# Last layer norm of a MoE transformer block: gain and bias moved from GpSimd to VectorE, row statistics from VectorE to ScalarE

## What is computed

```python
x1 = layer_norm(DEEPNORM_ALPHA * x + merged @ w_out[i], ln1_g[i], ln1_b[i])
y = hier_moe(x1, ...)     # y[token] = w0 * expert0(x1[token]) + w1 * expert1(x1[token])
ple = (p[i] @ w_ple[i]) * jax.nn.sigmoid(x1 @ w_ple_gate[i] + ple_gate_b[i])
x = layer_norm(DEEPNORM_ALPHA * x1 + y + ple, ln2_g[i], ln2_b[i])
# layer_norm: (x - mean) * rsqrt(mean((x - mean)^2) + 1e-5) * g + b, over the 1024 columns of a row
```

## Time and profile before

| what | value |
|---|---|
| median of 3 runs | 2067.24 us (2064.98 to 2072.45) |
| span of the profiled execution | 2062.2 us, first to last instruction |
| median of the runs less that span | 5.0 us |
| TensorE busy | 1806.4 us (88%) |
| VectorE busy | 1059.5 us (51%) |
| ScalarE busy | 826.6 us (40%) |
| GpSimd busy | 304.1 us (15%) |

### The profile page before, as it was taken

How to read it: one execution, slowest core, us unless ns; L and a number is a source line. 1 busy time by engine, 2 the same in 40 slices (tenths; PEclk the granted TensorE clock), 3 DMA queues, 4 the chain that set the end, 5 groups by cost and what they waited for, 6 DMA issues and landing times.

```text
span 2062.2 us, 27399 instructions
## 1 busy us (share of the span) xinstructions
PE 1806.4 (88%) x8478; PEld 1452.6 (70%) x8478; DVE 1059.5 (51%) x1307; ACT 826.6 (40%) x1077; POOL 304.1 (15%) x335
## 2 busy tenths in 40 slices
PE   7999999999988898989897898789888899899830
PEld 6888888888865586868676676677677677677720
DVE  2015655500125544243446634776776776777737
ACT  3132233211234313131213213666766766767621
POOL 0112212110100010000000120012221222111217
PEclk9999999999977898999999999899999999999965
DMA  6242333222423234242224266678878878888663
GB/s 233 87 118 106 121 115 114 98 78 92 150 98 116 94 114 142 92 158 92 87 104 136 81 209 250 269 314 342 358 305 349 348 309 362 329 333 360 263 239 128
DMA packets 100534, 396.62 MB, mean 192 GB/s; under 512 B 17921, under 2 KB 25345, under 8 KB 88194
## 3 DMA queue, kind: packets, MB, share of 16 engines
q1 hardware_dynamic: 77778, 319.45, 41.0%
q0 software_dynamic: 22704, 76.49, 9.8%
HBM read 331.01 MB, written 64.94 MB: 192 GB/s over the span
## 4 chain that ended last, share of the span: by engine, by line
PE 64%; DMA 9%; ACT 8%; DVE 8%; issue 6%; POOL 2%; ACTq 1%; SPq 0%; DVEq 0%; POOLq 0%
PE ps L796 42%; PE ps L1072 11%; DMA arena<-in_expert_w_up 6%; ACT act_h L1131 5%; PE ps L1088 2%; DVE act_l L1811 2%; PE ps L963 2%; PE ps L877 1%; PE ps L904 1%; ACT arena L1131 1%; PE ps L1039 1%; ACT blk_h L1131 1%; POOL arena L769 1%; DVE wgt_l L1452 1%; DVE blk_l L1818 1%
## 5 line engine op out<-in xcount | busy, mean ns | idle before, releaser
L1811 DVE TENSOR_TENSOR act_l<-arena,act_h 128x1024 fp32r<-128x1024 f32 x256 | 296.4, 1217 | 150.3 <-ACT act_h L1131 149.9
L1131 ACT ACTIVATE act_h<-arena 128x1024 fp32r (+2 forms) x280 | 266.9, 1025 | 159.6 <-DMA arena<-in_expert_w_up 146.1
L796 PE MATMUL ps<-act_h,wgt_h 128*128 128x512 f32 x768 | 304.7, 397 | 16.2 <-DVE act_l L1622 7.2
L796 PE MATMUL ps<-act_l,wgt_h 128*128 128x512 f32 x768 | 301.9, 393 | 0.0
L796 PE MATMUL ps<-act_h,wgt_l 128*128 128x512 f32 x768 | 301.4, 392 | 0.0
L1131 ACT ACTIVATE wgt_h<-arena 128x1024 fp32r (+3 forms) x220 | 222.8, 1032 | 188.8 <-PE ps L796 66.9
L1131 ACT ACTIVATE arena<-ps 128x512 f32<-128x512 f32 (+5 forms) x245 | 143.7, 605 | 354.9 <-PE ps L796 298.1
L796 PE MATMUL ps<-wgt_h,act_h 128*128 128x512 f32 (+1 forms) x640 | 249.6, 390 | 12.5 <-DVE act_l L1626 4.6
L1452 DVE TENSOR_TENSOR wgt_l<-arena,wgt_h 128x1024 fp32r<-128x1024 f32 (+2 forms) x92 | 102.7, 1144 | 293.5 <-ACT wgt_h L1131 289.1
L1131 ACT ACTIVATE arena<-arena 128x512 f32<-128x512 f32 (+4 forms) x131 | 82.1, 642 | 410.3 <-DVE arena L1494 121.3
L796 PE MATMUL ps<-wgt_l,act_h 128*128 128x512 f32 (+1 forms) x640 | 244.1, 381 | 0.0
(11 more groups left out here) (166 smaller groups left out, 2548.1 us busy)
## 6 DMA issues: line engine op xcount, KB each, us to landing
arena<-in_expert_w_gate SPq DMA_DIRECT2D x32, 2048.0 KB
arena<-in_expert_w_up SPq DMA_DIRECT2D x32, 2048.0 KB, 8.9
arena<-in_expert_w_down SPq DMA_DIRECT2D x32, 2048.0 KB, 13.1
arena<-in_w_in SPq DMA_DIRECT2D x13, 2048.0 KB, 9.6
z_t<-arena POOLq DMA_DIRECT2D x56, 256.0 KB, 2.3
arena<-z_t SPq DMA_DIRECT2D x40, 256.0 KB, 2.8
arena<-y_n SPq DMA_DIRECT2D x16, 512.0 KB, 5.4
kv_n<-arena POOLq DMA_DIRECT2D x24, 256.0 KB, 2.3
```

The lines of the kernel that those rows point to most:

```text
L796: ins = pe.matmul(out, left(x, k), right(y, k), start=k == 0 and (x, y) == (0, 0), stop=k == KC - 1 and x == 1)
L1131: return act.activation(out, in_, f, **kw)
L1811: dve.tensor_tensor(dst[:, w * c:w * (c + 1), :], arrived(src, m, b, slice(w * c, w * (c + 1))), f(high[:, w * c:w * (c + 1), :]), ALU.sub ...
```

## The change

GpSimd's eight tiles of gain and bias are taken out. VectorE's program for the stage is cut in three steps: `combined(t)` (both weighted sums, of which the second also gives the row sum through `accum_out`, and the negative mean), `scaled(t)` (reciprocal of the standard deviation, and minus mean times it) and `gained(t)` (gain, then bias). They run staggered: round i does `combined(i)`, `scaled(i-1)` and `gained(i-2)`, for ten rounds. ScalarE computes the sum of squared differences (`Square` with the negative mean as bias and `accum_out`), the square root with EPS as bias and 1/D as scale, and the same `Identity` as before. `bn_stats` and `bn_aggr` are gone.

```diff
-        fst, fmv = take(2, 2, 6), take(2, 2)
-        frs, fnm = take(2, 1), take(2, 1)
+        f_sum, f_mn, f_ss, f_sd, f_rs2, f_nm = (take(NT) for _ in range(6))
+        f_eps = take(1)
@@ sync
-                    sp.wait_ge(f_var, t + 1)
+                    sp.wait_ge(f_mean, t + 1)
@@ gpsimd
-            pool.wait_ge(l2_ld, 32)
-            for t in range(NT):
-                j = t % 2
-                pool.wait_ge(f_n, t + 1)
-                pool.tensor_tensor(zn[j], zn[j], l2g, ALU.mult).then_inc(f_g, 1)
-                pool.wait_ge(f_g, t + 1)
-                if t > 1:
-                    pool.wait_ge(f_st[j], 16 * (t // 2))
-                pool.tensor_tensor(zo[j], zn[j], l2b, ALU.add).then_inc(f_o[j], 1)
@@ scalar
+            def spread(t):
+                act.wait_ge(f_mean, t + 1)
+                if t > 1:
+                    act.wait_ge(f_o[t % 2], t // 2)
+                func(zn[t % 2], zt[t], ACT.Square, bias=f_mn[:, t:t + 1], accum_out=f_ss[:, t:t + 1]).then_inc(act_own, 1)
+                act.wait_ge(act_own, own.done())
+                func(f_sd[:, t:t + 1], f_ss[:, t:t + 1], ACT.Sqrt, scale=1.0 / D, bias=f_eps).then_inc(f_sq, 1)
+
+            def normed(t):
+                act.wait_ge(f_rs, t + 1)
+                func(zn[t % 2], zt[t], ACT.Identity, bias=f_nm[:, t:t + 1], scale=f_rs2[:, t:t + 1]).then_inc(f_n, 1)
             for t in range(NT):
-                j = t % 2
-                act.wait_ge(f_var, t + 1)
-                func(frs[:, j, :], frs[:, j, :], ACT.Sqrt).then_inc(f_sq, 1)
-                if t > 1:
-                    act.wait_ge(f_g, t - 1)
-                    act.wait_ge(f_o[j], t // 2)
-                act.wait_ge(f_rs, t + 1)
-                func(zn[j], zt[t], ACT.Identity, bias=fnm[:, j, :], scale=frs[:, j, :]).then_inc(f_n, 1)
+                spread(t)
+                normed(t)
@@ vector
+            dve.memset(f_eps, EPS).then_inc(dve_own, 1)
+            dve.wait_ge(dve_own, own.done())
             dve.wait_ge(z_ld, 16 * NT)
-            for t in range(NT):
...
+            def combined(t):
+                k = t % (NT // 2)
+                dve.wait_ge(f_z[k], 32 * (t // (NT // 2) + 1))
+                dve.scalar_tensor_tensor(zt[t], y0[k], slot_w[:, 0, t:t + 1], zt[t], ALU.mult, ALU.add).then_inc(dve_own, 1)
+                dve.wait_ge(dve_own, own.done())
+                dve.scalar_tensor_tensor(zt[t], y1[k], slot_w[:, 1, t:t + 1], zt[t], ALU.mult, ALU.add,
+                                         accum_out=f_sum[:, t:t + 1]).then_inc(dve_own, 1)
+                dve.wait_ge(dve_own, own.done())
+                dve.tensor_scalar(f_mn[:, t:t + 1], f_sum[:, t:t + 1], -1.0 / D, None, ALU.mult).then_inc(f_mean, 1)
+
+            def scaled(t):
+                dve.wait_ge(f_sq, t + 1)
+                dve.reciprocal(f_rs2[:, t:t + 1], f_sd[:, t:t + 1]).then_inc(dve_own, 1)
+                dve.wait_ge(dve_own, own.done())
+                dve.tensor_tensor(f_nm[:, t:t + 1], f_mn[:, t:t + 1], f_rs2[:, t:t + 1], ALU.mult).then_inc(f_rs, 1)
+
+            def gained(t):
                 j = t % 2
+                dve.wait_ge(f_n, t + 1)
+                if t == 0:
+                    dve.wait_ge(l2_ld, 32)
+                dve.tensor_tensor(zn[j], zn[j], l2g, ALU.mult).then_inc(dve_own, 1)
                 dve.wait_ge(dve_own, own.done())
                 if t > 1:
+                    dve.wait_ge(f_st[j], 16 * (t // 2))
+                dve.tensor_tensor(zo[j], zn[j], l2b, ALU.add).then_inc(f_o[j], 1)
+            for t in range(NT + 2):
+                if t < NT:
+                    combined(t)
+                if 0 < t <= NT:
+                    scaled(t - 1)
+                if t > 1:
+                    gained(t - 2)
```

More of the change, by code:

```diff
@@ L325, in build @@
                              "y_done", "y_evacuated", "slots_y_stored"))
-        l2_ld, z_ld, f_g, f_z = sem("ln2_ld"), sem("z2_ld"), sem("f_gained"), sems("y_ld", NT // 2)
-        f_var, f_sq, f_rs, f_n, f_o = sem("f_var"), sem("f_sqrt"), sem("f_rstd"), sem("f_normed"), sems("f_out", 2)
+        l2_ld, z_ld, f_z = sem("ln2_ld"), sem("z2_ld"), sems("y_ld", NT // 2)
+        f_mean, f_sq, f_rs, f_n, f_o = sem("f_mean"), sem("f_std"), sem("f_rstd"), sem("f_normed"), sems("f_out", 2)
         f_st = sems("f_stored", 2)
```

## The result

The changed kernel took 2047.07 us (median of four runs, 2046.24 to 2051.30), the kernel before 2067.01 us on the same occasion: ratio 0.9907, 95% interval 0.9891 to 0.9922, some 19 us less. The forecast was 2052.9 us with a range that began at 2048.

What follows compares the result with a forecast made beforehand. The prediction took the final stage's chain to run through GpSimd and a ScalarE piece, with VectorE and GpSimd holding each other up. The stage takes 47.1 instead of 61.4 us, so 2067.24 - 14.3 = 2052.9 us, range 2048 to 2063.

Steps and rivals of the forecast that it cites:

- VectorE's loss comes from GpSimd and goes with it: Final stage, per tile: VectorE loses 2.12 us on line 1876 beside GpSimd's addition, and the change removes that loss.
- A full round is 5.63 us: VectorE's middle rounds: combined 2.94, scaled 0.28 and gained 2.41 us, against 7.15 us per tile before.
- The first two rounds: Stage start: round 0 ends at 1998.18, combined(1) at 2001.12, and scaled(0) at 2001.5 us after a 0.07 us wait.
- The table load: ScalarE, tile 0: one load of 1.28 us behind the first Square, making VectorE wait 0.07 us for the square root.
- Rounds 8 and 9: Stage end: round 8, without a combined to hide under, takes 4.5 us, and round 9 takes 2.41 us.
- The 5.6 us behind the last addition stay: End of the program: a store and the program's end, 5.6 us, unchanged.
- The median less the span, 5.0 us, carried over: Whole kernel: the median of the runs is 5.0 us above the profiled span, and this difference stays unchanged.
- First rival: VectorE's accumulating operation in combined takes two passes, 1.30 us more per tile; gain 5.1 us, time 2062.1 us; chance 0.11.
- The rule of the Trainium skill that was weighed: VectorE's combined: scalar_tensor_tensor with two non-bf16 SBUF sources halves its throughput, making the accumulating half twice as long.
- Second rival: ScalarE: Square and Sqrt have no common table, so two loads per tile; time 2056 to 2066 us; chance 0.05.
- Third: VectorE's accumulating operation runs at a quarter of the pace, 3.9 us more per tile; time 2083 us; chance 0.03.
- fourth: VectorE's 2.12 us losses per tile are not due to GpSimd and stay; no gain, 2067 us; chance 0.03.

Runs made afterwards that it cites:

- one-input: Kernel before, with line 1876's small operation written as a tensor_scalar with one tensor input; ratio to the kernel before 0.9983, stage 59.22 us.
- PSUM kernels: Kernel before, with line 1876 taking one tensor input and each tile's first weighted sum written to PSUM; ratio to the kernel before 0.9959, stage 51.10 us.
- own-buffer kernel: Changed kernel, with Square writing its own buffer and Square of tile t + 1 ahead of Identity of tile t; ratio to the kernel before 0.9894.
- late-memset: Changed kernel, with one 128x1 GpSimd memset added behind the last addition; ratio to the kernel before 0.9920, end 5.79 us.
- last-tile kernels: Kernel before, with gain and bias of only tile 7 moved from GpSimd to VectorE; ratio to the kernel before 0.9982, end 3.13 us.
- second measurement: Changed kernel run again without an edit; ratio to the kernel before 0.9926, stage 45.71 us.
- statistics-only kernel: Changed kernel without gained: only the statistics move to ScalarE, gain and bias stay on GpSimd; ratio to the kernel before 0.9968, stage 56.80 us.

## Why the prediction was right and wrong

- *VectorE's loss comes from GpSimd and goes with it*: right, but the picture behind it was not. The text counted 2.12 us per tile as lost by VectorE and 0.94 by GpSimd, as two engines that hold each other up. The runs show one shared resource whose time was full: the earlier trace rows is its schedule, 2.59 + 2.34 + 2.34 us per tile. The Trainium skill, "SBUF — State Buffer", section "Who interferes with whom", says that a VectorE instruction with two SBUF inputs and a GpSimd instruction that reads SBUF lock each other out. The one-input and PSUM kernels agree, with 7.03 and 5.71 us per tile.
- *A full round is 5.63 us*: mis-sized by 0.26, measured 5.37. The accumulated sum cost 0.02 to 0.03 on the path instead of 0.17 with its gap (line 1861 begins at 2019.54 and line 1864 at 2020.87, 1.33 us later), since its 0.08 us row overlaps the end of the operation. The first weighted sum starts 0.08 us ahead of the addition's end (2023.60 against 2023.67), an overlap I had granted to `scaled` and `gained` alone. Over six rounds this is 1.5 us.
- *The first two rounds*: 6.39 us against 6.3 worked out. The pair of tile 1 landed 0.6 us late; I had allowed nothing. The table load, put on the path for 0.07 us, cost nothing behind that wait: the square root of tile 0 was ready at 2006.62 and the reciprocal began at 2007.06. So round 1 had no wait for the square root, against what was expected.
- *Rounds 8 and 9*: 6.93 us against 6.9. The exposed wait for the square root was there, and the own-buffer kernel removes it. That the figure fits so well is in part luck: `Square` took 1.15 us and not 1.24, and `Sqrt` 0.29 and not 0.20.
- *The 5.6 us behind the last addition stay*: this is the step that failed most, by 2.56 us; the runs show 3.08 us in its place. I took it for a store and the end of the program. A row of line 98 would have told: GpSimd's DRAIN until 2062.0, 2.5 us behind SyncE's. The step failed because I costed an engine's removed work and not what its queue does at the end. The late-memset and last-tile kernels show it both ways: with GpSimd's last operation at the end 5.79 us, with it moved ahead 3.13.
- *The median less the span, 5.0 us, carried over*: this mixed two things. In the profiled execution of the changed kernel the time is 1.6 us above its span (2051.3 less 2049.7), and in all executions of all kernels here it is 1.5 to 2.8 us above. The rest of 5.0 was the difference between one execution and the median.
- Stage and end together are 18.2 us where I had 14.3. That puts the time at 2067.2 - 18.2 = 2049.0 us, inside the range; the last 2 us to 2047.07 lie within the scatter of executions, and the second measurement (2053.88, beside 2067.53 for the kernel before) lies on the other side.
- *First rival, two passes for the accumulating operation*: did not happen, 1.28 us. The rule of the Trainium skill that was weighed ("Vector Engine (DVE) Microarchitecture Reference", "Points that are easy to get wrong") is contradicted for the accumulating form too: two float32 SBUF sources, 1285 ns.
- *Second rival, two tables*: did not happen, one load. *Third and fourth*: did not happen.
- *Both halves are needed*, which the prediction did not say. Alone, gain and bias bring 4.8 us of stage and the statistics 4.6, together 9.3; the change brings 15.7. With only the one, VectorE's own sum is 7.06 us per tile; with only the other, the port's sum less its overlaps is 6.69. Each half by itself runs into the other limit.

## What to carry to other kernels

Where VectorE and GpSimd work side by side, add up what needs the shared way into SBUF (two-input VectorE operations and GpSimd's) as if it were one engine, and try moving an input to PSUM before moving work (8.1 us of stage here). Cost the end of the program by the closing row of each queue, not as a constant: the last small operation on GpSimd can set it (2.7 us here). When a round gets shorter, work out again every wait that was called hidden.

## What the hardware showed that was not expected

- GpSimd's closing DRAIN ended 5.4 us behind its last operation, with a 128x1024 addition (kernel before), and a 128x1 memset of 0.10 us alike. In the changed kernel, where an indirect DMA is its last operation (it ends at 1989.2), the DRAIN ended 9.6 us behind.
- The lock is by operand, not by size: 128x1 operations with two SBUF inputs took 2.28 us (line 1876) and 1.40 us (line 1881 in the statistics-only kernel) instead of 0.16, and the one-input form of line 1876 took 0.21 beside GpSimd's addition.
- At a change of hands the two engines overlap by some 0.14 us (6.69 us per tile against a sum of 7.24, over four changes).
- Reading out an accumulator took 0.08 us on VectorE, and 0.19 us on ScalarE; `Sqrt` on 128x1 with a scale and a bias by row took 0.29 us against 0.20 without.
